# A two-layer diffusion backbone step on one core: the opening norm deferred tile by tile, weight panels loaded and awaited in another order

## The reference

```
for layer in 0, 1:                                  # mixer: differential attention, then MLA
  mod = SiLU(cond) @ w_mod + b_mod                  # 9 vectors of 1024, one set per token group
  x = x + mod[2] * 0.5 * swiglu(rms(x)*g*(1+mod[1]) + mod[0])      # FFN 0: w_in 1024x5632, w_out 2816x1024
  x = x + mod[5] * mixer(rms(x)*g*(1+mod[4]) + mod[3])
  x = x + mod[8] * 0.5 * swiglu(rms(x)*g*(1+mod[7]) + mod[6])      # FFN 1
```

## Time and profile before

| | us |
|---|---|
| median of 3 runs | 1517.96 |
| lowest, highest | 1517.74, 1518.47 |
| profiled execution, its own time | 1518.2 |
| its span, first to last instruction | 1515.8 |
| PE busy | 1508.3 |
| DVE busy | 1087.1 |
| ACT busy | 668.1 |

### The profile page before, as it was taken

One profiled execution on the slowest core, in us unless ns is written; L12 is line 12 of the kernel. 1 busy time (PEld: TensorE's weight loads), 2 busy tenths in 40 slices (PEclk: granted clock), 3 DMA queues, 4 the chain that ended last, 5 costly groups with the idle time before them and its releaser, 6 DMA issues.

```text
span 1515.8 us, 22012 instructions
## 1 busy us (share of the span) xinstructions
PE 1508.3 (100%) x8886; PEld 1446.7 (95%) x8886; DVE 1087.1 (72%) x1747; ACT 668.1 (44%) x1031; POOL 34.8 (2%) x45
## 2 busy tenths in 40 slices
PE   9999999999999999999999999999999999999999
PEld 5999999988889999999999999999997899999999
DVE  5887887789887887876678787877578876343332
ACT  5433333254686633333363333325458765333221
POOL 0000000000031000000000000000020000000000
PEclk9999999999999999999999999999999999999999
DMA  9756566543233365655455655654331033333233
GB/s 391 280 211 233 207 247 223 188 153 116 94 98 139 126 232 201 241 195 184 165 186 190 227 214 213 231 185 152 116 124 57 3 137 112 139 113 137 100 131 118
DMA packets 52276, 258.00 MB, mean 170 GB/s; under 512 B 6608, under 2 KB 8912, under 8 KB 37072
## 3 DMA queue, kind: packets, MB, share of 16 engines
q1 hardware_dynamic: 49632, 253.13, 46.2%
q10 hardware_dynamic: 2544, 3.48, 0.7%
HBM read 253.29 MB, written 3.29 MB: 169 GB/s over the span
## 4 chain that ended last, share of the span: by engine, by line
PE 96%; DVE 1%; DMA 1%; ACT 1%; issue 1%; SPq 0%; DVEq 0%; ACTq 0%
PE ps L2178 30%; PE ps L2180 29%; PE ps L2179 29%; PE ps L2830 1%; DMA wm_first<-in_w_mod_first 1%; PE ps L2721 1%; PE ps L2839 1%; PE ps L2853 1%; PE ps L2576 1%; PE ps L2545 1%; PE ps L2287 0%; PE ps L2505 0%; PE ps L2310 0%; PE ps L2563 0%; PE ps L2228 0%
## 5 line engine op out<-in xcount | busy, mean ns | idle before, releaser
L1375 DVE TENSOR_TENSOR w_lo<-w_raw,w_hi 128x2048 fp32r<-128x2048 f32 (+3 forms) x177 | 347.3, 1964 | 233.8 <-ACT w_hi L799 231.5
L2178 PE MATMUL ps<-hx_hi,w_hi 128*128 128x384 f32 (+1 forms) x1432 | 480.2, 335 | 0.0
L2179 PE MATMUL ps<-hx_lo,w_hi 128*128 128x384 f32 (+1 forms) x1432 | 478.6, 334 | 0.0
L2180 PE MATMUL ps<-hx_hi,w_lo 128*128 128x384 f32 (+1 forms) x1432 | 478.5, 334 | 0.0
L799 ACT ACTIVATE w_hi<-w_raw 128x2048 fp32r<-128x2048 f32 (+3 forms) x177 | 292.7, 1654 | 407.1 <-DMA w_raw<-in_w_out 210.7
L2178 PEld LDWEIGHTS ps<-hx_hi,w_hi 128*128 128x128 f32 x1432 | 268.9, 188 | 2.3 <-issue 1.8
L2179 PEld LDWEIGHTS ps<-hx_lo,w_hi 128*128 128x128 f32 x1432 | 268.9, 188 | 0.0
L2180 PEld LDWEIGHTS ps<-hx_hi,w_lo 128*128 128x128 f32 x1432 | 268.8, 188 | 0.0
L2180 PE MATMUL ps<-g_hi,w_lo 128*128 128x384 f32 x704 | 236.6, 336 | 0.0
L2178 PE MATMUL ps<-g_hi,w_hi 128*128 128x384 f32 x704 | 236.5, 336 | 0.0
L2179 PE MATMUL ps<-g_lo,w_hi 128*128 128x384 f32 x704 | 236.5, 336 | 0.0
(11 more groups left out here) (293 smaller groups left out, 1501.3 us busy)
## 6 DMA issues: line engine op xcount, KB each, us to landing
w_raw<-in_w_in SPq DMA_DIRECT2D x88, 1024.0 KB, 4.8
wm<-in_w_mod SPq DMA_DIRECT2D x128, 512.0 KB, 5.7
w_raw<-in_w_out SPq DMA_DIRECT2D x64, 704.0 KB, 4.1
w_raw<-in_w_qkv SPq DMA_DIRECT2D x12, 1024.0 KB, 4.8
wm_first<-in_w_mod_first SPq DMA_DIRECT2D x8, 1024.0 KB, 19.0
w_raw<-in_w_o SPq DMA_DIRECT2D x7, 1024.0 KB, 4.8
w_raw<-in_w_qup SPq DMA_DIRECT2D x8, 576.0 KB, 3.7
w_raw<-in_w_down SPq DMA_DIRECT2D x6, 704.0 KB, 4.0
```

The source lines that it names most:

```text
L1375: nc.vector.tensor_tensor(w_lo[:, slot, 0:width], w_raw[:, slot, 0:width], w_hi[:, slot, 0:width].bitcast(F32), ALU.subtract).then_inc(w_l ...
L2178: nc.tensor.matmul(out, l_hi, r_hi, start=first, stop=False)
L2179: nc.tensor.matmul(out, l_hi, r_lo, start=False, stop=False)
L2180: return nc.tensor.matmul(out, l_lo, r_hi, start=False, stop=last)
```

## The change

It makes the first norm (n = 0) a deferred one, too, and works on it k tile by k tile.

- **SP.** The first slice of `w_mod_first` is asked for before x; x comes in three parts and panels 0 and 1 in four quarters of columns, one quarter of both panels per DMA, between the slices. For this the columns of w_in are laid out k by k (tile t = 2k + half instead of 8*half + k).
- **PE.** 3 filler matmuls instead of 9, and 2 more behind the first columns. `plain` (k = 0, 1) takes `xg_raw`, the others `hx_hi`, `hx_lo` holding xg, each with the two shift columns. The sum of squares and the broadcast move from the beginning to k = 3 and 4.
- **ACT, DVE.** Per tile k: `xg_first(k)` and, from k = 2, `first_xg_low(k)`. The normalised h (for panels 2 to 21) is made besides; h_high(k) overwrites xg of tile k and waits until PE has used it. Behind it come the halves of panels 2 and 3, two `scale_out`, and `first_panels`: the SiLU, product and split of panels 0 and 1, as in the other deferred norms. Only then come the seven parameter DMAs, then the loop from m = 2. SiLU of `cond` goes into m = 2.
- **Panels.** PE waits for panel m = 2 of the first FFN and panel m = 3 of all four in halves (k < 4, then the rest). Modulation tiles are asked for only behind panel 4's load (n > SLOTS), and none is consumed before m = 3; the units moved from w_in 0 go to five panels of w_out 0.

```diff
     if name == "in":
-        return {0: 3, 1: 3 if m > 2 else 0, 2: 3 if m > 2 else 0, 3: 0}[f]
-    return {0: 2 if m < 15 else 0, 1: 2 if m in (6, 10) else 1, 2: 2 if m < 14 else 0, 3: 0}[f]
+        return {0: (2 if m < 5 else 4 if m > 9 and m % 2 == 0 else 3) if m > 2 else 0, 1: 3 if m > 2 else 0, 2: 3 if m > 2 else 0, 3: 0}[f]
+    return {0: 3 if m in (1, 3, 5, 7, 13) else 2 if m < 15 else 0, 1: 2 if m in (6, 10) else 1, 2: 2 if m < 14 else 0, 3: 0}[f]
...
-        DEFER = {2: 0, 3: 1, 5: 2}
+        DEFER = {0: 0, 2: 1, 3: 2, 5: 3}
...
# SP
+            load_first(0)
+            load_x(slice(0, 2), first_in[0])
+            load_quarter(0)
+            load_first(1)
+            load_first(2)
+            load_x(slice(2, 4), first_in[1])
+            load_quarter(1)
+            load_first(3)
+            load_x(slice(4, KD), x_in)
+            load_first(4)
+            load_quarter(2)
+            load_first(5)
+            load_first(6)
+            load_quarter(3)
+            load_first(7)
             load(2, "in", 0, 2)
...
-                    while asked < MODS and (MOD_AT[asked] <= n + 3 or asked < FIRST_MODS + WM_SLOTS) and (
+                    while n > SLOTS and asked < MODS and (MOD_AT[asked] <= n + 3 or asked < FIRST_MODS + WM_SLOTS) and (
...
# ACT
+                def xg_first(k):
+                    if k == 0:
+                        act.wait_ge(first_in[0], 32)
+                    act.wait_ge(gains, 2 * k + 2)
+                    out = xg_raw[:, k, :] if k < RAW else hx_hi[:, k, :]
+                    nc.scalar.activation(out[:, T:T + 2], modc[:, k, :], ACT.Copy)
+                    for s, seg in SEGS:
+                        ins = nc.scalar.activation(out[:, seg], x[:, k, seg], ACT.Copy, scale=gmul[:, k, s:s + 1])
+                    ins.then_inc(xg_hi_done, 1)
...
+                to_high(2)
+                high_half(2, 0)
+                xg_first(7)
+                high_half(2, 1)
                 for k in range(3, KD):
-                    copied(k)
                     to_tile(k)
-                    h_high(0, k)
-                high_half(2, 0)
-                high_half(2, 1)
+                    to_high(k)
+                high_half(3, 0)
+                high_half(3, 1)
+                first_panels(0, 0)
...
             first_norm()
-            act.wait_ge(cond_in, 16)
-            nc.scalar.activation(cond[:], cond[:], ACT.Silu).then_inc(cond_ready, 1)
+            act.wait_ge(h_lo_done, h_val(0, KD - 1))
             for dst, name in ((ropes, "ropes"), (gq, "gq"), (gm, "gm"), (gmT, "gmT"), (subg, "subg"), (gdown, "gdown"),
                               (lamp, "lamp")):
                 act.dma_start(dst[:] if name != "lamp" else dst, d[name]).then_inc(params_in, 16)
-            ffn_in(0)
+            ffn_in(0, 2)
...
# DVE, the end of first_norm
+                first_xg_low(7)
                 low_half(2, 0)
+                scaled(0, 5)
+                context(0, 5, 0)
+                h_low(0, 3)
                 low_half(2, 1)
+                scaled(0, 6)
+                h_low(0, 4)
+                scaled(0, 7)
+                context(0, 7, 0)
+                h_low(0, 5)
+                h_low(0, 6)
+                h_low(0, 7)
+                scale_out(0, 0, 0)
+                low_half(3, 0)
+                low_half(3, 1)
+                scale_out(0, 0, 1)
+                first_panels(0)
...
# PE, the opening
+                    pe.wait_ge(dve_consts, 1)
+                    zeros(3)
                     pe.wait_ge(condT_ready, 1)
+                    pe.wait_ge(dve_consts, 4)
                     mod_rows(0)
                     mod_columns(0)
+                    zeros(2)
+                    plain(0, 0, 0)
...
+                    mod_rows(7)
+                    tile(1, 5, 0)
+                    tile(1, 5, 1)
+                    mod_columns(7)
+                    tile(0, 6, 0)
+                    tile(0, 6, 1)
+                    tile(1, 6, 0)
+                    tile(1, 6, 1)
+                    for m in range(2):
                         for half in range(2):
+                            tile(m, 7, half)
                 for m in range(2, KF):
-                    pe.wait_ge(w_lo_done, base + m + 1)
+                    halves = n in DEFER and m == 3 or n == 0 and m == 2
+                    if halves:
+                        pe.wait_ge(half_lo, HALF_NO[base + m] + 1)
+                    else:
+                        pe.wait_ge(w_lo_done, base + m + 1)
```

More of the change, by code:

```diff
@@ L122, in build_step @@
         hx_hi = sb("hx_hi", [P, KD, TX], F32R)
+        with ExitStack() as part:
+            xg_raw = sb("xg_raw", [P, 2, TX], where=part)
         with ExitStack() as part:
@@ L910, in to_tile, with first_high @@
+                def first_high(q):
+                    for m in range(2):
+                        if m == 0:
+                            act.wait_ge(first_in[q], 32 if q < 2 else 16)
+                        nc.scalar.activation(w_hi[:, m, quarter(q)], w_raw[:, m, quarter(q)], ACT.Copy).then_inc(
+                            w_hi_done if q == 3 else half_hi, 1)
                 def to_tile(k):
                     latents(0, k, gmul[:, k, 1:2], modc[:, k, 1:2])
-                copied(0)
-                high_half(0, 0)
@@ L915, in first_norm, with to_high @@
-                high_half(0, 1)
+                    if k % 2 == 0:
+                        contexts(0, k, gmul[:, k, 0:1], modc[:, k, 0:1])
+                def to_high(k):
+                    if k < KD - 1:
+                        act.wait_ge(xg_used, xg_uses(0, k))
+                    else:
+                        act.wait_ge(panel_used, 2)
+                    h_high(0, k)
+                copied(0)
+                xg_first(0)
+                square(0)
+                square(1)
+                copied(1)
@@ L983, in ffn_in @@
                         high(base + m + 2)
+                    if f == 0 and m == start:
+                        act.wait_ge(cond_in, 16)
+                        nc.scalar.activation(cond[:], cond[:], ACT.Silu).then_inc(cond_ready, 1)
                     act.wait_ge(panel_used, base + m + 1)
@@ new lines, in first_xg_low @@
+                def first_xg_low(k):
+                    v.wait_ge(xg_hi_done, xg_val(0, k))
+                    nc.vector.tensor_tensor(hx_lo[:, k, T:T + 2], modc[:, k, :], hx_hi[:, k, T:T + 2].bitcast(F32),
+                                            ALU.subtract)
+                    xg_low(0, k)
+                v.wait_ge(small_in, 32)
+                gains_of(0)
+                add(1)
+                gains_of(1)
+                add(2)
+                add(3)
+                gains_of(2)
@@ L1653, in ffn_in @@
                         low(base + m + 2)
+                    if f == 0 and m == start:
+                        v.wait_ge(cond_ready, 1)
                     units = mod_units("in", f, m)
@@ new lines, in plain, with tile @@
+                        t = 2 * k + half
+                        mm = nc.tensor.matmul(ps[:, bank_pair(m) + half, 0:T + 2], w_raw[:, m, t * P:(t + 1) * P],
+                                              xg_raw[:, k, 0:T + 2], start=k == 0, stop=False)
+                        if m == 1 and half:
+                            mm.then_inc(xg_used, 1)
+                    def tile(m, k, half):
+                        if half == 0:
+                            if m == 0:
+                                pe.wait_ge(xg_lo_done, xg_low_val(0, k))
+                            if k == 6:
@@ L2395, in ffn_in @@
                             pe.wait_ge(h_lo_done, h_val(n, k))
+                        if halves and k == KD // 2:
+                            pe.wait_ge(w_lo_done, base + m + 1)
                         mm = part(m, k)
```

290 lines of the change are left out of this document (152 added, 138 removed).

## The result

The changed kernel takes 1523.09 us (median of 6 runs, 1521.59 to 1524.13), against 1518.22 for the kernel before on the same chip (6 runs): ratio 1.0031 [1.0019, 1.0044]. The forecast was 1519.1 with a range up to 1521.2; the time lies 1.9 us outside, on the slow side. By the medians the kernel is 0.3% slower, more than the 0.2% that the prediction took for a difference; to that it had given 0.12. The profiled execution is the slowest of the six, 1524.13, with a span of 1522.2.

The account below looks back on a forecast made before the run. The prediction took PE's work, laid end to end, to bound the kernel. It added +0.65 (panel 4's later start) and +0.5 (PE's clock level) to the median 1517.96, giving 1519.1 us, range 1515.4 to 1521.2.

Parts of the forecast that it names:

- the stall at panel 4: First FFN, panel 4: PE waits 2.3 us for its remainder, starting at 62.4 against 61.76 before, +0.65 us.
- (d): Sign at panel 4: seven issues behind the second g_hi, w_hi 0.1 behind the last, PE waiting about 2.3 us for w_lo.
- the walk: The prediction's step-by-step timing of PE, ACT and DVE from the opening to panel 4; about 0.6 us uncertain.
- PE's own order, -1.65: Opening to panel 4: what PE's order alone allows, panel 4 at 60.1, 1.65 us earlier than before.
- +0.5 for PE's level in the opening: Opening: half of the 1.05 us lost if PE is still at 1.2 GHz and rows(0) takes 2.1 instead of 1.07.
- (a): Sign in the opening: first row matmuls near 6.65, taking 1.07 or 2.1 us together.
- Rival 2: Opening, rows(0) to plain(1,0,0): PE's lower clock level lasts, panel 4 at 64.9, 1521.1 us; 17 in 100.
- (b): Sign in the opening: plain(0,0,0) near 10.2 to 11.3, rows(7) near 35 to 36.
- (c): Sign late in the opening: PE idle about 1.2 us before tile(0,7,0), released by DVE's hx_lo.
- (f): Sign in the rest: no PE wait for w_lo or wm, taking 1454.0 us as before.
- (e): Sign in the first FFN: panel 4 starts at 62.4 to 63.5.
- Rival 1: Panel 4: issues covered, or DVE and ACT over 2 us sooner; start at 60.1, -1.65, 1516.3 us; 27 in 100.

Follow-up runs that it names:

- e1: The changed kernel with the seven parameter DMAs issued on ACT behind high(4) and SiLU of cond instead of behind the second g_hi; 1517.59 us.
- e5: e1 with the four quarter DMAs of panels 0 and 1 joined into two, with rows of 4 KB instead of 2 KB; 1518.81 us.
- e2: The changed kernel with five fp32 filler matmuls on PE ahead of its wait for panel 4's remainder, stall kept; 1521.14 us.
- e7: e1 with PE waiting for the whole of panels 2 and 3 instead of half by half; 1519.10 us.
- e3: The kernel before with only the change's panel and modulation part, nothing of the opening; 1518.07 us, ratio 0.9998.
- e8: e1 with tile 7's gain product ahead of ACT's half panel, and three more moves for tile 7 on DVE and PE; 1516.67 us.
- e11: The changed kernel with two of the seven parameter DMAs (gdown, lamp) moved behind SiLU of cond, five left ahead of high(4); 1520.19 us.
- e12: e8 with slice 4 asked for ahead of the last part of x, and squares, sum and broadcast moved back; 1520.95 us.
- e9: e8 with the joined quarter DMAs of e5; 1518.34 us, ratio 1.0000.

## Why the prediction was wrong, step by step

The step that failed is the pricing of the stall at panel 4. The prediction counted the stall alone (2.3 us, panel 4 at 62.4) and put what follows it at nothing, without a reason. The runs show a stall of 3.2 us behind an opening that was itself 1.5 late (panel 4 at 64.86), and 2.8 us of slow matmuls behind it.

- **The step that was to decide did decide** (d): the seven issues right behind g_hi, w_hi of panel 4 right behind the last, PE waiting for w_lo. e1 shows it by taking it away. It was mis-sized. From g_hi(1) to high(4) were 3.3 - 0.05 = 3.25 us in the walk (54.9 to 58.15) and 4.42 in the trace (56.15 to 60.57). I had taken the sum of the seven issues in their old place, 3.2; here they end 4.3 after they begin, with gm at 1.18 and gdown at 0.81. The term was 1.2 us short; why these two issues took longer here is open.
- **PE's own order, -1.65, was 0.14.** Panel 4 was due at 61.62, not 60.1. All of these 1.5 us are there at rows(7) (36.66 for 35.1), and none is added behind it. Between plain(0,0,0) and rows(7) PE needs 26.4 us: 1.94 are waits (0.37, 0.55 and 1.02 for slice 4) where I had 1.2, and 24.5 are work where I had 23.7: the sum and the broadcast took 1.3 for 0.9, the eight plain 5.8 for 5.5. Slice 4 lands at 24.65 where the walk's rate gives 23.3, and slice 7 at 34.8 instead of 33.6. The landings were 1.2 us later than costed, and e5 gives no sign that the short rows of the quarters are why. Only slice 4 reached PE, by its wait of 1.02; for slice 7 it did not wait. The chain of DVE and ACT came 1.25 late with it (g_hi(1) at 56.15 for 54.9), so the stall (64.86 - 61.62 = 3.2 for 2.3) grew by the longer issues less 0.3.
- **The missing term: +2.8** (1.95 on the medians). PE, idle for 3.09 us, came back at 1.2 GHz. I weighed this clock for the start of the kernel only, and at the place where I myself had put a stall of 2.3 us I priced the stall and not what follows it. This took the time out of the range: e2, without it, is at 1521.14, at the range's end.
- **+0.5 for PE's level in the opening was 0**: rows(0) took 1.07 (a). Rival 2's place and mechanism did not occur in this execution; that its time (1521.1) lies nearest to the measured one is luck. Its price was wrong as well. The prediction said that a slow rows(0) moves all behind it, since PE is the bound. In e2, whose opening is the same, rows(0) did run slow:

```profile
6.39 1.62 PE L2417 MATMUL ps<-wm_first,mod_prod 128*32 128x256 f32 x16 [0.27 <-DMA wm_first<-in_w_mod_first]
```

  There plain(0,0,0) starts at 10.62 for 10.24, but rows(4) at 24.70 for 24.71 and panel 2 at 44.95 for 44.97: the waits for hx_lo and for slice 4 took the delay up.
- **Right:** (b) plain(0,0,0) at 10.24; (c) the 1.2 us before tile(0,7,0), by hx_lo; awaiting panel 2 whole costs 1.5 (e7); panels and modulation at nothing (e3); the rest after panel 4 as before but for the slow stretch and 0.55 us (f); rows of the table put it at 1453.7 to 1454.4. (e), panel 4 at 62.4 to 63.5, failed: 64.86.
- Rival 1 (issues covered) is what e1 made: the forecast for it was 1516.3; it gives 1517.59, because panel 4 starts at 61.76 for 60.1; the time outside the span, 0.5 shorter, gives part of that back.

## What to carry to other kernels

The seven DMAs issued from ACT's queue were free only where ACT had long work already handed over (e1); ask at each place what stands behind the issues. Where a forecast has an idle TensorE, price the time at 1.2 GHz that may follow as well as the wait. Where the wait can't be removed, try filling it: in e2 that gave back 1.95 of the 5.5 us. The best version here, e8, leaves the change as it is but for the place of seven DMAs and the order around one tile. It is faster than both kernels, by 0.1% than the kernel before.

## What the runs showed of the hardware that was not expected

- The same DMA issue on ACT's queue took more than twice as long in one kernel as in another: gm 1.18 us in the changed kernel and 0.46 in e1, where gq took 1.04 for 0.45. Open.
- The fall to 1.2 GHz is not told by the length of one wait. It came after an idle 3.09 us in the changed kernel's profiled execution, after 1.46 in e11's opening and 1.34 in e12's; it did not come after 1.45 in e8's opening, nor after 1.94 in e9's opening, nor after 1.68 in e11's panel 4 behind dense work. It was back at 2.4 GHz 3 to 4 us later in the two openings and about 6 us after the restart in panel 4. What sets it off, and why it differs between executions of one kernel, stays open.
- In 5 to 9 us the DMA engines, at a busy share of 0.96 to 0.98, moved 363 and 293 GB/s in the changed kernel, against 401 and 440 before. Open.
- The time outside the span is 1.9 to 2.0 us in every run of a kernel with the new opening, and 2.4 to 2.5 in the median in the two without (2.2 to 2.6 in single runs). About half of e1's gain over the kernel before is this. Why is open.
